# Long convolutions as 128-by-32 points in half-array tile pairs, in one phase, with the filters generated early

## The chip, the cores and the metric

The kernel runs on one core of a Trainium2 chip. The metric is the device time of one execution in microseconds (us); before the change it is 2717.03 us, the median of three runs (2716.83 to 2722.48).

## What is computed

An encoder block on 2048 tokens of 1024 columns, in float32. What matters here is the Hyena half: two-sided long filters of 4096 points for 512 channels are generated by a small network, and two long convolutions with gates follow one another.

```python
h = (z @ fw3).reshape(seq, 2, HY_ORDER, D_HY) * exp(-t * deltas)
k = concatenate([hf, 0, hb[1:][::-1]])
k = k / (sum(abs(k), axis=0) + EPS);  kf = rfft(k)            # 4096 points
z = x1 * (irfft(rfft(v, 4096) * kf[:, 0])[:2048] + v * skip[0])
z = x2 * (irfft(rfft(z, 4096) * kf[:, 1])[:2048] + z * skip[1])
```

Ahead of it stand a norm and the input projection with a recurrent unit (LRU), behind it the output projection, the router, 32 experts and the final sum.

## The kernel before, in words

The kernel is a chain of phases. Each clears its semaphores (`PhaseSemaphores.begin`), runs one instruction stream per engine, and ends when the last of its transfers has landed; nothing of the next begins before. Order inside a phase is written out by hand, with semaphores; DMAs are issued by SyncE (SP) and ScalarE (ACT), each in its own order.

1. `load_and_norm` (L83) normalizes and transposes x to `hT`, and runs the filter network's first two layers; their result `zz` goes to DRAM (L131).
2. `project_and_lru` (L226) makes 5 column groups for each of 4 channel groups (640 products of 512 columns in `fill`, L361), the short convs on DVE (`conv`, L474), the LRU, and transposes (L376) into DRAM `L`.
3. `filters` (L529) has 32 iterations of two orders: a spread of zz (POOL, L582), a generating product (PE, L609), times the decay (DVE, L660), absolute value (DVE, L663), its sum (POOL, L589), a first-stage transform (PE, L615), eviction (ACT, L639), and a store to `KA`. The reciprocals of the sums (`invn`) come last.
4. For each of two orders: `conv_forward` (L671), 16 tiles by two halves of 64-point transforms (L693), evicted to `stage` and stored to `SA` in 2 MB pieces, POOL multiplying by skip beside it (L714); `conv_blocks` (L717), 32 block transforms, each with a forward product of the signal and two of the filter (L758), two elementwise products (DVE, L803) and two inverse products (L763, L764), with matrices and data read by SP, and results stored to `SI` by ACT; `conv_inverse` (L806), which loads `SI` back in 2 MB pieces (L831), makes two products per tile (L840, L841), scales (DVE, L869), adds the skip part (POOL, L862) and gates (DVE, L876), and for the second order also squares (ACT, L902), transposes (PE, L847) and stores to `YT`.
5. `output_projection` (first DMA at L1032), `route`, `experts`, `combine`.

All transform products are full-array f32 products of 128 rows, 128 columns of weights and 512 streamed columns. Each is two LDWEIGHTS and two MATMUL records in the trace.

## Time and profile before

| | |
|---|---|
| median of 3 runs | 2717.03 us (2716.83 to 2722.48) |
| profiled execution, its own time | 2722.55 us |
| its span, mean granted clock | 2720.8 us, 0.933 |
| busy: PE, PE weight load, DVE, ACT, POOL | 2319.1, 1455.2, 1418.7, 1067.5, 316.8 us |
| DMA | 531.74 MB, 195 GB/s over the span |

The span is the time from the first to the last instruction. Busy shares are means over stages with different limits, so they are read by stage. PEclk is the granted TensorE clock as a share of full speed. In a timeline, a row gives start, busy time, engine, line, operation, output<-input and count; what stands in brackets is the idle time before it and what ended it.

### The profile page before, as it was taken

To read this page: it belongs to the slowest core of one execution; us is meant where nothing else is said; L and a number is where in the kernel's file an instruction comes from. 1 tells how busy PE (TensorE), PEld (TensorE's weight loads), DVE (VectorE), ACT (ScalarE), POOL (GpSimd) and SP (SyncE) were. 2 spreads that over 40 slices of the span, in tenths; PEclk is the share of its full clock that TensorE was granted. 3 is DMA by queue.
4 is the path that set the end of the run, shared out by engine and by line. 5 is a ranking of instruction groups with operands and counts; after the bars stand their busy time and mean duration, and the time that the engine had idled before them with its cause. 6 is when DMAs were issued, how large, how long until landed. Compare 5 with 4: busy or idle time off the path is not lost. (4 is left out here: it accounts for less than half of the span.)

```text
span 2720.8 us, 33071 instructions
## 1 busy us (share of the span) xinstructions
PE 2319.1 (85%) x8253; PEld 1455.2 (53%) x8254; DVE 1418.7 (52%) x1238; ACT 1067.5 (39%) x1342; POOL 316.8 (12%) x337
## 2 busy tenths in 40 slices
PE   2699999999879599679849994699999999999940
PEld 1344444444333244234327873588878788788830
DVE  4357291745679123312244445446486864655447
ACT  4232221414122322032222221456586965766533
POOL 0000000000078300420120000000000000000023
PEclk8899999999989799789869997799999999999975
DMA  3122313121266488378743431667598986786648
GB/s 152 34 79 64 100 47 108 33 73 58 62 214 217 173 276 280 143 276 290 276 173 111 153 136 57 246 230 290 220 388 310 395 310 240 277 309 217 261 185 355
DMA packets 263770, 531.74 MB, mean 195 GB/s; under 512 B 27311, under 2 KB 98195, under 8 KB 259347
## 3 DMA queue, kind: packets, MB, share of 16 engines
q1 hardware_dynamic: 221812, 390.76, 41.1%
q10 hardware_dynamic: 30112, 97.53, 9.0%
q0 software_dynamic: 11808, 43.00, 4.2%
q8 instruction: 17, 0.28, 0.0%
q14 instruction: 21, 0.17, 0.0%
HBM read 390.69 MB, written 140.51 MB: 195 GB/s over the span
## 5 line engine op out<-in xcount | busy, mean ns | idle before, releaser
L361 PE MATMUL pj<-hT,W 128*128 128x512 f32 x1280 | 553.7, 594 | 2.7 <-DMA W<-in_w_in_dram 2.7
L361 PEld LDWEIGHTS pj<-hT,W 128*128 128x128 f32 x1280 | 243.0, 191 | 304.3 <-issue 304.3
L1458 PE MATMUL p<-wh_hi,x_hi 128*128 128x512 f32 x768 | 309.0, 402 | 11.2 <-DVE wh_lo L1583 11.1
L1583 DVE TENSOR_TENSOR wh_lo<-w_raw,wh_hi 128x2048 fp32r<-128x2048 f32 x128 | 284.8, 2287 | 51.5 <-ACT wh_hi L1547 48.8
L1458 PE MATMUL p<-wh_lo,x_hi 128*128 128x512 f32 x768 | 304.2, 396 | 0.0
L1458 PE MATMUL p<-wh_hi,x_lo 128*128 128x512 f32 x768 | 304.1, 396 | 0.0
L1547 ACT ACTIVATE wh_hi<-w_raw 128x2048 fp32r<-128x2048 f32 x128 | 234.7, 1914 | 0.3 <-DMA w_raw<-in_exp_w_dram 0.2
L803 DVE TENSOR_TENSOR u<-pr,zs 128x512 f32<-128x512 f32 x64 | 44.3, 692 | 287.4 <-ACT zs L778 167.5
L1458 PEld LDWEIGHTS p<-wh_hi,x_hi 128*128 128x128 f32 x768 | 144.6, 188 | 49.5 <-DVE wh_lo L1583 15.0
L1458 PEld LDWEIGHTS p<-wh_hi,x_lo 128*128 128x128 f32 x768 | 144.7, 188 | 35.0
L1458 PEld LDWEIGHTS p<-wh_lo,x_hi 128*128 128x128 f32 x768 | 144.8, 189 | 32.7
L1458 PE MATMUL pyy<-wy_hi,a_hi 128*128 x392 | 160.0, 408 | 2.3 <-ACT yb L1529 2.3
L1458 PE MATMUL pyy<-wy_lo,a_hi 128*128 x392 | 155.5, 397 | 0.0
L1458 PE MATMUL pyy<-wy_hi,a_lo 128*128 x392 | 155.3, 396 | 0.0
L1583 DVE TENSOR_TENSOR wy_lo<-w_raw,wy_hi 128x2048 fp32r<-128x2048 f32 x64 | 143.6, 2285 | 0.0
L1594 DVE TENSOR_TENSOR a<-p,s 128x512 f32<-128x512 f32 x48 | 33.2, 692 | 204.2 <-ACT s L1556 204.2
L406 ACT ACTIVATE hraw<-pj 128x512 f32<-128x512 f32 x48 | 28.7, 597 | 265.1 <-PE pj L361 265.1
L1547 ACT ACTIVATE wy_hi<-w_raw 128x2048 fp32r<-128x2048 f32 x64 | 119.3, 1911 | 2.4 <-DMA w_raw<-in_exp_w_dram 1.5
L1428 POOL COPY curidx<-idx 128x1 int32 (+1 forms) x50 | 9.1, 183 | 870.3 <-PE px L1466 795.3
L1556 ACT ACTIVATE s<-p 128x512 f32<-128x512 f32 x48 | 28.9, 601 | 207.6 <-PE p L1458 207.3
L758 PE MATMUL pz<-zin,mats 128*128 128x512 f32 x128 | 67.9, 613 | 32.8 <-DMA kin<-scratch_KA 32.8
L783 ACT ACTIVATE qo<-pq 128x512 f32<-128x512 f32 x64 | 38.2, 597 | 139.0 <-PE pq L764 139.0
(266 smaller groups left out, 3796.2 us busy)
## 6 DMA issues: line engine op xcount, KB each, us to landing
w_raw<-in_exp_w_dram SPq DMA_DIRECT2D x512, 256.0 KB, 4.6
w_raw<-in_exp_w_dram SPq DMA_DIRECT2D x128, 512.0 KB, 9.6
scratch_YB<-yb ACTq DMA_DIRECT2D x50, 512.0 KB
mats<-in_mats_dram SPq DMA_DIRECT2D x64, 320.0 KB, 3.2
scratch_YB<-zero SPq DMA_DIRECT2D x4, 4096.0 KB, 14.6
scratch_KA<-kst ACTq DMA_DIRECT2D x32, 512.0 KB, 3.5
scratch_SA<-stage ACTq DMA_DIRECT2D x8, 2048.0 KB, 6.7
zin<-scratch_SA SPq DMA_DIRECT2D x64, 256.0 KB, 4.1
```

What stands on the lines that cost most here:

```text
L361: last = pe.matmul(pj[n][:, :], lhs(k), rhs(k, n), start=(k == 0), stop=(k == n_k - 1))
L406: ins = act.activation(out(n), pj[n][:, :], func)
L758: pe.matmul(bank_[s % 2][:, :], mats[:, s, m, :], rhs[:, s, :], start=True, stop=True).then_inc(fwd, 1)
L783: act.activation(qo[:, s, :], pq[s % 2][:, :], ACT.Copy).then_inc(q_evac, 1)
L803: dve.tensor_tensor(dst[:, s % 2, :], src[s % 2][:, :], zs[:, s % 2, :], ALU.mult).then_inc(uv_ready, 1)
L1428: pool.tensor_copy(cur[:, :], idx[:, ds(B + LEAD, 1)]).then_inc(idx_ready, 1)
L1458: mm = pe.matmul(acc[:, :], x[:, k, :], w, start=(k == 0 and i == 0), stop=(k == n - 1 and i == 2))
L1547: act.activation(place, raw[:, j:j + 2, :], ACT.Copy).then_inc(rounded, 1)
L1556: act.activation(s1[:, :], p1[:, :], ACT.Silu).then_inc(s_ready, 1)
L1583: dve.tensor_tensor(lo, raw[:, j:j + 2, :], hi.bitcast(F32), ALU.subtract).then_inc(lowered, 1)
L1594: dve.tensor_tensor(a[:, :], p3[:, :], s1[:, :], ALU.mult).then_inc(a_ready, 1)
```

## The change

- The 4096 points are split as N1 = 128 by N2 = 32 instead of 64 by 64. The first stage is one 128-point transform. A signal has 64 nonzero rows, so its first stage (`spread`) is two products with 64 rows each, one on partitions 0 to 63 and one on 64 to 127, into two PSUM banks. The last stage (`collect`) is two products with 64 columns of weights each, one into PSUM partitions 0 to 63 and one into 64 to 127.
- The block stage works on 16 pairs per order: for filter and signal 4 products each of 128 rows by 64 columns (2 parts by 2 halves), for the inverse 4 of 64 rows by 128 columns. The filter is transformed with the same matrix as the signal, and the complex product is done by DVE (two products of 1024 columns and a sum) and POOL (a difference). All 32 forward and 16 by 2 inverse matrices are kept on chip, loaded once.
- Both orders run in one phase, `conv`, unrolled. Collecting order 0 and spreading order 1 are interleaved tile by tile. All DMAs of the phase are issued by SP. Block data move in pieces of 256 KB, the stage in pieces of 2 MB; L is read through a ring of three 1 MB buffers.
- The skip term is added to the filter's point 0 (`norm`, `kt0`), and 1/sum is multiplied into the short conv's weights and biases, so the skip pass, the scaling and the sum on the output go.
- `filters` runs before `project_and_lru`, unrolled, on `zzd`, which `load_and_norm` leaves on chip; the absolute value goes from DVE to ACT.
- The short convs write their result in the order of even and odd positions; output projection and combine read x and write out in the matching order.

```diff
-HALF = R // 2
+N1, N2 = P, N // P
+HALF = N1 // 2
+PAIRS = N2 // 2
...
-            sp.wait_ge(mlp_sin, BASE + 3)
-            sp.dma_start(dram["ZZ"], zz[:, :]).then_inc(zz_out, 16)
...
+            act.activation(zzd[0:R, 0, :], arg[0:R, :], ACT.Sin).then_inc(mlp_sin, 1)
+            act.activation(zzd[R:P, 1, 1:SEQ][:, ::-1], arg[R:P, 1:SEQ], ACT.Sin).then_inc(mlp_sin, 1)
...
+            dve.memset(zzd[R:P, 0, :], 0.0)
+            dve.memset(zzd[0:R, 1, :], 0.0)
+            dve.memset(zzd[R:P, 1, 0:1], 0.0)
...
+            taps = PT[:, Q_HW:Q_HB, :].rearrange("p (t w) c -> p t w c", w=3)[:, :, 1:3, :]
+            step(dve.tensor_tensor(taps, taps, invn[:, :, :].unsqueeze(1).broadcast_to([P, 3, 2, CT]), ALU.mult))
+            step(dve.tensor_tensor(PT[:, Q_HB + 1:Q_HB + 3, :], PT[:, Q_HB + 1:Q_HB + 3, :], invn[:, :, :], ALU.mult))
+            by_parity = lambda a: a.rearrange("p (m g) -> p g m", g=2)
-                    conv(step, hc[:, slot, :], hraw[:, slot, :], 3, Q_HW + which, 3, Q_HB + which, hc_ready)
+                    conv(step, hc[:, slot, :].rearrange("p (g m) -> p g m", g=2), hraw[:, slot, :],
+                         3, Q_HW + which, 3, Q_HB + which, hc_ready, by_parity)
...
+def filters(nc, dram, zzd, invn):
...
+            def store(i):
+                sp.wait_ge(kst_ready, i + 1)
+                sp.dma_start(dram["KA"][:, :, order[i], :].rearrange("o p c -> p o c"), kst[:, i % 4]).then_inc(kst_out[i % 4], 16)
+            def generate(j):
+                if j >= 2:
+                    pe.wait_ge(k_ready, j - 1)
+                for o in range(2):
+                    last = pe.matmul(pk[j % 2][:, o, :], view[:, j], w3[:, o, :], start=True, stop=True)
+                last.then_inc(kgen, 1)
+            def transform(i):
+                j = order[i]
+                if j:
+                    pe.wait_ge(k_ready, j + 1)
+                else:
+                    pe.wait_ge(k0_ready, 1)
+                if i >= 2:
+                    pe.wait_ge(kst_ready, i - 1)
+                for o in range(2):
+                    last = pe.matmul(pa[i % 2][:, o, :], fa[:, :], tile(j)[:, o, :], start=True, stop=True)
+                last.then_inc(fa_done, 1)
+            generate(0)
+            generate(1)
+            for j in range(2, N2):
+                generate(j)
+                transform(j - 2)
...
+            for o in range(2):
+                pe.matmul(pk[0][:, o, :], ones[:, :], acc[:, o, :], start=True, stop=True)
+            for o in range(2):
+                for c in range(CT):
+                    place = (o * CT + c) * 2
+                    last = pe.matmul(pk[1][:, 0, place:place + 2], acc[:, o, c * P:(c + 1) * P], ones[:, 0:2], start=True, stop=True)
+            last.then_inc(norm_mm, 1)
+            transform(N2 - 1)
+            def magnitude(j):
+                act.wait_ge(k_ready, j + 1)
+                if j >= 2:
+                    act.wait_ge(summed, j)
+                act.activation(ka[:, j % 2], tile(j), ACT.Abs).then_inc(abs_ready, 1)
+            def evacuate(i):
+                act.wait_ge(fa_done, i + 1)
+                if i >= 4:
+                    act.wait_ge(kst_out[i % 4], 16 * (i // 4))
+                act.activation(kst[:, i % 4], pa[i % 2][:, :, :], ACT.Copy).then_inc(kst_ready, 1)
...
+                pool.tensor_tensor(acc[:, :, :], acc[:, :, :], ka[:, j % 2], ALU.add).then_inc(summed, 1)
...
+                dve.tensor_tensor(tile(j), pk[j % 2][:, :, :], dec[:, j % 4, :].unsqueeze(1).broadcast_to([P, 2, CH]), ALU.mult).then_inc(k_ready, 1)
...
+            dve.scalar_tensor_tensor(out=norm[:, :, :], in0=pk[0][0:1, :, :], scalar=EPS, in1=skip[:, :, :], op0=ALU.add, op1=ALU.mult).then_inc(norm_ready, 1)
...
+def conv(nc, dram, rB, ident):
...
+        def rows(a, p, t):
+            first = (p & 1) * 64 + (p >> 1 & 1) * 32 + t * 16 + (p >> 2)
+            return a[first:first + 13:4]
+            def load_k(n):
+                for t in range(2):
+                    sp.dma_start(kin[:, n % 3, t, :], rows(dram["KA"][n // PAIRS], n % PAIRS, t)).then_inc(kin_in[n % 3], 16)
+            def load_z(n):
+                for t in range(2):
+                    sp.dma_start(zin[:, n % 3, t, :], rows(dram["SA"][n // PAIRS], n % PAIRS, t)).then_inc(zin_in[n % 3], 16)
+            def store_q(n):
+                sp.wait_ge(q_evac, n + 1)
+                for t in range(2):
+                    sp.dma_start(rows(dram["SI"][n // PAIRS], n % PAIRS, t), qo[:, n % 2, t, :]).then_inc(q_out[n % 2], 16)
+            def save_stage(o, g):
+                sp.wait_ge(a_act, NT * o + 4 * g + 4)
+                sp.wait_ge(a_dve, NT * o + 4 * g + 4)
+                sp.dma_start(dram["SA"][o][:, 8 * g:8 * g + 8, :], stage[:, 8 * g:8 * g + 8, :]).then_inc(sa_out, 16)
+            def load_stage(o):
+                for s in range(2):
+                    sp.wait_ge(q_out[s], 32 * (PAIRS // 2) * (o + 1))
+                for g in range(4):
+                    sp.dma_start(stage[:, 8 * g:8 * g + 8, :], dram["SI"][o][:, 8 * g:8 * g + 8, :]).then_inc(si_in[g], 16)
+            def blocks(o):
+                sp.wait_ge(sa_out, 64 * (o + 1))
+                for n in range(o * PAIRS, o * PAIRS + 3):
+                    load_z(n)
+                for n in range(o * PAIRS, o * PAIRS + PAIRS):
+                    sp.wait_ge(z_mm, 2 * n + 2)
+                    if n + 3 < (o + 1) * PAIRS:
+                        load_z(n + 3)
+                    if n + 3 < 2 * PAIRS:
+                        sp.wait_ge(k_mm, n + 1)
+                        load_k(n + 3)
+                    if n > o * PAIRS:
+                        store_q(n - 1)
+                store_q((o + 1) * PAIRS - 1)
+            sp.dma_start(fs[:, :], dram["fa_signal"]).then_inc(tables_in, 16)
+            load_ring(0)
+            load_ring(1)
+            sp.dma_start(ia[:, :], dram["inv_a"]).then_inc(tables_in, 16)
+            load_ring(2)
+            sp.dma_start(fwd[:, :, :], dram["fwd_b"]).then_inc(fwd_in, 16)
+            for n in range(3):
+                load_k(n)
+            for g in range(GROUPS):
+                sp.wait_ge(a_mm, 8 * g + 8)
+                load_ring(g + 3)
+                save_stage(0, g)
+            sp.dma_start(inv[:, :, :, :], dram["inv_b"]).then_inc(inv_in, 16)
+            blocks(0)
+            load_stage(0)
+            for g in range(GROUPS):
+                sp.wait_ge(gated, 4 * g + 4)
+                load_ring(g + 7)
+                save_stage(1, g)
+            blocks(1)
+            load_stage(1)
+            sp.wait_ge(gated, NT + 4)
+            load_ring(11)
...
+            def spread(bank, t, src, free):
+                if free > 0:
+                    pe.wait_ge(a_act, free)
+                    pe.wait_ge(a_dve, free)
+                for g in range(2):
+                    h = slice(g * HALF, g * HALF + HALF)
+                    pe.matmul(bank[:, g, :], fs[h, :], src[h], start=True, stop=True).then_inc(a_mm, 1)
+            def k_product(n):
+                p = n % PAIRS
+                pe.wait_ge(kin_in[n % 3], 32 * (n // 3) + 32)
+                if n >= 2:
+                    pe.wait_ge(prod, 2 * n - 2)
+                for r in range(2):
+                    for t in range(2):
+                        h = slice(t * HALF, t * HALF + HALF)
+                        last = pe.matmul(pk[n % 2][h, r, :], fwd[:, 2 * p + t, r * HALF:r * HALF + HALF], kin[:, n % 3, t, :], start=True, stop=True)
+                last.then_inc(k_mm, 1)
+            def z_product(n):
+                p = n % PAIRS
+                pe.wait_ge(zin_in[n % 3], 32 * (n // 3) + 32)
+                if n:
+                    pe.wait_ge(zs_ready, 2 * n)
+                for r in range(2):
+                    for t in range(2):
+                        h = slice(t * HALF, t * HALF + HALF)
+                        last = pe.matmul(pz[h, r, :], fwd[:, 2 * p + t, r * HALF:r * HALF + HALF], zin[:, n % 3, t, :], start=True, stop=True)
+                    last.then_inc(z_mm, 1)
+            def inverse(n):
+                p = n % PAIRS
+                pe.wait_ge(yr_ready, n + 1)
+                if n:
+                    pe.wait_ge(q_evac, n)
+                for r, y, done in ((0, yr, yr_ready), (1, yi, yi_ready)):
+                    pe.wait_ge(done, n + 1)
+                    for t in range(2):
+                        h = slice(t * HALF, t * HALF + HALF)
+                        last = pe.matmul(pq[:, t, :], inv[h, p, r, :], y[h, n % 2, :], start=(r == 0), stop=(r == 1))
+                last.then_inc(inv_mm, 1)
+            def blocks(o):
+                first = o * PAIRS
+                k_product(first)
+                for n in range(first, first + PAIRS):
+                    z_product(n)
+                    if n + 1 < first + PAIRS:
+                        k_product(n + 1)
+                    if n > first:
+                        inverse(n - 1)
+                inverse(first + PAIRS - 1)
+            def collect(o, out, l, free):
+                if l % 4 == 0:
+                    pe.wait_ge(si_in[l // 4], 16 * (o + 1))
+                if free > 0:
+                    pe.wait_ge(gated, free)
+                for g in range(2):
+                    h = slice(g * HALF, g * HALF + HALF)
+                    last = pe.matmul(out[h, :], ia[:, :], stage[:, 2 * l + g, :], start=True, stop=True)
+                last.then_inc(i_mm, 1)
...
+            LAG = 2
+            for l in range(NT + LAG):
+                if l < NT:
+                    collect(0, pq[:, l % 2, :], l, l - 1)
+                if l >= LAG:
+                    t = l - LAG
+                    pe.wait_ge(gated, t + 1)
+                    spread((pz, *pk)[t % 3], t, z[:, t % 4, :], NT + t - 2 if t >= 3 else 0)
...
+            def evacuate(bank, n, t):
+                act.wait_ge(a_mm, 2 * n + 1)
+                act.activation(stage[:, 2 * t, :], bank[:, 0, :], ACT.Copy).then_inc(a_act, 1)
+            def signal(n):
+                for r in range(2):
+                    act.wait_ge(z_mm, 2 * n + r + 1)
+                    if n >= 2:
+                        act.wait_ge(prod, 2 * n - 2)
+                    act.activation(zs[:, n % 2, r, :], pz[:, r, :], ACT.Copy).then_inc(zs_ready, 1)
+            def result(n):
+                act.wait_ge(inv_mm, n + 1)
+                if n >= 2:
+                    act.wait_ge(q_out[n % 2], 32 * (n // 2))
+                act.activation(qo[:, n % 2], pq[:, :, :], ACT.Copy).then_inc(q_evac, 1)
...
+                dif = pool.tensor_tensor(yr[:, n % 2, :], by_r[:, n % 2, 0, :], by_i[:, n % 2, 1, :], ALU.subtract)
...
+                    dve.tensor_tensor(out[:, n % 2], pk[n % 2][:, :, :], zs[:, n % 2, r, :].unsqueeze(1).broadcast_to([P, 2, CH]), ALU.mult).then_inc(prod, 1)
...
+                both = dve.tensor_tensor(yi[:, n % 2, :], by_r[:, n % 2, 1, :], by_i[:, n % 2, 0, :], ALU.add)
...
+            with ExitStack() as early:
+                zzd = sb(early, "zzd", [P, 2, SEQ])
+                load_and_norm(nc, dram, hT, zzd, ident)
+                filters(nc, dram, zzd, invn)
+            project_and_lru(nc, dram, hT, invn, ident)
+        conv(nc, dram, rB, ident)
```

## Rows read from the trace of the kernel before

**Rows 1.** Busy time by stage: stretch, its length, engines, clock, DMA share, GB/s.

```profile
96.00:749.00 653.00, 628.25 (x1601) 290.00 (x1601) 354.16 (x151) 165.44 (x226) 0.93 (x3) 0.98 0.23 68
749.00:903.00 154.00, 123.69 (x260) 48.35 (x260) 132.13 (x134) 38.23 (x64) 109.34 (x98) 0.92 0.57 202
903.00:946.50 43.50, 30.23 (x64) 13.00 (x64) 0.00 (x0) 18.46 (x32) 20.31 (x16) 0.81 0.50 202
```

**Rows 2.** Timeline of TensorE in the first block phase, and that phase's middle by engine.

```profile
968.05 1.02 PE L758 MATMUL pr<-kin,mats 128*128 128x512 f32 x2
968.91 1.02 PE L758 MATMUL pi<-kin,mats 128*128 128x512 f32 x2
...
955.00:1090.00 135.00, 135.00 (x311) 59.45 (x311) 41.26 (x63) 37.02 (x62) 0.00 (x0) 0.99 0.83 275
```

**Rows 3.** Timeline at the seams of the phases, and one restart by engine.

```profile
749.70 0.34 SPq L560 DMA_DIRECT2D zz<-scratch_ZZ  x1
...
903.69 0.34 SPq L683 DMA_DIRECT2D faz<-in_fa_signal_dram  x1
...
952.90 2.07 PE L758 MATMUL pz<-zin,mats 128*128 128x512 f32 x2 [16.47 <-DMA kin<-scratch_KA]
954.76 1.91 PE L758 MATMUL pr<-kin,mats 128*128 128x512 f32 x2
...
1092.51 1.02 PE L764 MATMUL pq<-v,mats 128*128 128x512 f32 x2
1107.01 2.04 PE L840 MATMUL py<-stage,ia 128*128 128x512 f32 x2 [13.47 <-DMA stage<-scratch_SI]
...
1191.45 2.07 PE L758 MATMUL pz<-zin,mats 128*128 128x512 f32 x2 [16.33 <-DMA kin<-scratch_KA]
...
1397.54 2.12 SPq L1032 DMA_DIRECT2D wo<-in_w_out_dram  x4
...
1104.00:1109.00 5.00, 1.99 (x3) 0.99 (x4) 0.00 (x0) 0.00 (x0) 0.00 (x0) 0.50 1.01 429
```

**Rows 4.** Timeline of one iteration of the filter loop.

```profile
803.73 1.51 DVE L663 SCALAR_TENSOR_TENSOR ka<-kt 128x512 f32<-128x512 f32 x1
803.75 1.12 PE L615 MATMUL pa<-kt,fa 128*128 128x512 f32 x2 [0.35 <-DVE kt L660]
804.71 1.88 PE L609 MATMUL pk<-w,zb 128*128 128x512 f32 x4
805.57 0.19 PEld L609 LDWEIGHTS pk<-w,zb 128*128 128x128 f32 x1 [0.24 <-issue]
...
807.80 1.12 PE L615 MATMUL pa<-kt,fa 128*128 128x512 f32 x2 [0.35 <-DVE kt L660]
```

**Rows 5.** Groups of instructions: count, busy us and mean ns, idle before.

```profile
L803 DVE TENSOR_TENSOR u<-pr,zs 128x512 f32<-128x512 f32 x64 | 44.3, 692 | 287.4 <-ACT zs L778 167.5 <-PE pr L758 119.8
L500 DVE TENSOR_TENSOR Ib<-Ib,xc 128x2048 f32<-128x2048 f32 x4 | 9.2, 2294 | 0.1
L1655 ACT ACTIVATE outt<-xcomb 128x1024 f32<-128x1024 f32 x16 | 16.9, 1056 | 34.0 <-DMA out_dram<-outt 31.6 <-DVE xcomb L1671 2.3
L783 ACT ACTIVATE qo<-pq 128x512 f32<-128x512 f32 x64 | 38.2, 597 | 139.0 <-PE pq L764 139.0
L589 POOL TENSOR_TENSOR acc<-acc,ka 128x512 f32<-128x512 f32 x64 | 81.1, 1267 | 24.3 <-DVE ka L663 24.3
L1064 POOL TENSOR_TENSOR sq<-sq 128x256 f32<-128x256 f32 x16 | 11.7, 733 | 217.5 <-ACT sq L1125 217.5
```

**Rows 6.** Timeline of the start and of one channel group of the projection.

```profile
19.71 2.97 DVE L170 TENSOR_SCALAR arg<-flat,vec 128x512 f32<-128x512 f32 x4 [16.35 <-PE flat L203]
...
403.68 4.74 DVE L479 SCALAR_TENSOR_TENSOR hc<-hraw,par,hc 128x2048 f32<-128x2048 f32 x2
...
422.08 1.96 PE L376 MATMUL tr<-ident,hc 128*128 128x128 f32 x16
```

**Rows 7.** Timeline of the second inverse phase: the four transposes of one tile.

```profile
1370.78 0.60 PE L847 MATMUL pt<-ident,zn 128*128 128x128 f32 x4
```

More of the change, by code:

```diff
@@ new lines, in _ @@
+            for j in range(N2):
+                if j >= 4:
+                    sp.wait_ge(k_ready, j - 3)
+                sp.dma_start(dec[:, j % 4, :], dram["decay"][:, j, :]).then_inc(dec_in[j % 4], 16)
+                if j >= 6:
+                    store(j - 6)
+            for i in range(N2 - 6, N2):
+                store(i)
+            for s in range(4):
+                sp.wait_ge(kst_out[s], 16 * (N2 // 4))
+        @block.tensor
+        def _(pe):
+            pe.wait_ge(par_in, 16 * N_PAR)
+            view = zzd.rearrange("p h (q l) -> p l h q", l=N2)
+            def generate(j):
[20 more added lines that the diff above has]
+                transform(j - 2)
+            transform(N2 - 2)
+            pe.wait_ge(k_ready, N2)
+            pe.wait_ge(summed, N2 + 1)
+            for o in range(2):
[6 more added lines that the diff above has]
+            transform(N2 - 1)
@@ new lines, in _ @@
+        @block.scalar
+        def _(act):
+            def magnitude(j):
[8 more added lines that the diff above has]
+                act.activation(kst[:, i % 4], pa[i % 2][:, :, :], ACT.Copy).then_inc(kst_ready, 1)
+            magnitude(0)
+            magnitude(1)
+            for j in range(2, N2):
+                magnitude(j)
+                evacuate(j - 2)
+            evacuate(N2 - 2)
+            evacuate(N2 - 1)
@@ new lines, in _ @@
+            sp.dma_start(inv[:, :, :, :], dram["inv_b"]).then_inc(inv_in, 16)
[9 more added lines that the diff above has]
+            load_ring(11)
+            for t in range(NT):
+                sp.wait_ge(zt_ready, t + 1)
+                sp.dma_start(dram["YT"][t, :, 4:8, :].rearrange("p c n -> p (c n)"), zt[:, t % 2, :]).then_inc(zt_out[t % 2], 16)
@@ new lines, in _ @@
+            pe.wait_ge(tables_in, 32)
+            for l in range(NT):
+                if l % 4 == 0:
+                    pe.wait_ge(ring_in[l // 4 % 3], 16 * (l // 12) + 16)
+                spread((*pk, pz, pq)[l % 4], l, ring[:, l // 4 % 3, l % 4, :], l - 3)
+            pe.wait_ge(fwd_in, 16)
+            pe.wait_ge(a_act, NT)
+            pe.wait_ge(a_dve, NT)
+            pe.wait_ge(inv_in, 16)
+            blocks(0)
+            LAG = 2
[6 more added lines that the diff above has]
+                    spread((pz, *pk)[t % 3], t, z[:, t % 4, :], NT + t - 2 if t >= 3 else 0)
@@ new lines, in _ @@
+            pe.wait_ge(a_act, 2 * NT - 2)
+            pe.wait_ge(a_dve, 2 * NT - 2)
+            blocks(1)
+            LAG = 3
+            for l in range(NT + LAG):
+                if l < NT:
+                    collect(1, pk[l // 2 % 2][:, l % 2, :], l, NT + l - 3 if l >= 4 else 0)
+                if l >= LAG:
+                    t = l - LAG
+                    pe.wait_ge(gated, NT + t + 1)
+                    if t >= 2:
+                        pe.wait_ge(zt_ready, t - 1)
+                    for q in range(4):
+                        last = pe.transpose(pz[:, t % 2, q * P:(q + 1) * P], z[:, t % 4, q * P:(q + 1) * P], ident[:, :])
+                    last.then_inc(tr, 1)
@@ L696, in _ @@
         @block.scalar
         def _(act):
-            with act.Fori(0, NT // 4) as it:
-                for s in range(4):
-                    for h in range(2):
-                        act.wait_ge(mm, BASE + it * 8 + 2 * s + h + 1)
-                        act.activation(stage[:, h, ds(it * 4 + s, 1), :].rearrange("p a c -> p (a c)"), pa[s][h][:, :], ACT.Copy).then_inc(evac, 1)
-                act.wait_ge(evac, BASE + it * 8 + 8)
-                four = lambda a: a[:, :, ds(it * 4, 4), :].rearrange("p h l c -> p h (l c)")
-                act.dma_start(four(dram["SA"]), four(stage)).then_inc(stored, 16)
@@ new lines, in result, with blocks @@
+            def result(n):
[3 more added lines that the diff above has]
+                act.activation(qo[:, n % 2], pq[:, :, :], ACT.Copy).then_inc(q_evac, 1)
+            def blocks(o):
+                first = o * PAIRS
+                for n in range(first, first + PAIRS):
+                    signal(n)
+                    if n > first:
+                        result(n - 1)
+                result(first + PAIRS - 1)
@@ new lines, in _ @@
+            for l in range(NT):
+                evacuate((*pk, pz, pq)[l % 4], l, l)
+            blocks(0)
+            for l in range(NT):
+                evacuate((pz, *pk)[l % 3], NT + l, l)
+            blocks(1)
+            for t in range(NT):
+                act.wait_ge(gated, NT + t + 1)
+                if t:
+                    act.wait_ge(squared, t)
+                act.activation(junk[:, :], z[:, t % 4, :], ACT.Square, accum_out=ssq[:, t:t + 1]).then_inc(squared, 1)
+            act.wait_ge(ms, 2)
@@ new lines, in gate @@
+            def gate(out, t, G0, free):
+                G = G0 + t // 4
+                dve.wait_ge(i_mm, (G0 // GROUPS - 1) * NT + t + 1)
+                dve.wait_ge(ring_in[G % 3], 16 * (G // 3) + 16)
+                if t >= 4:
+                    dve.wait_ge(free, 2 * (NT + t - 3) if free is a_mm else t - 3)
+                dve.tensor_tensor(z[:, t % 4, :], out, ring[:, G % 3, t % 4, :], ALU.mult).then_inc(gated, 1)
+            for l in range(NT):
+                evacuate((*pk, pz, pq)[l % 4], l, l)
```

536 lines of the change are left out of this document (163 added, 373 removed).

## The prediction

> **What bounds the kernel now.** I read the page first: TensorE is busy for 85% of the span and no other engine for more than 52%. The table of engines by stage then shows where it is not: from 749 to 1397 us, the filters and the six conv phases, the reader sees PE short of full in the filters and, with a granted clock of 0.81, in the first forward phase, and full in the projection [rows 1]. That is the stretch the change replaces. Elsewhere it touches little. The timeline of TensorE inside a block phase gives the unit of all that follows: a f32 product of 512 columns is two MATMUL records, starts 0.858 us after the one before it, and its records end 0.16 us after the next has started [rows 2]. Five such products per transform make 4.29 us, and 32 of them 137 us: the block phases are bound by TensorE, with DMA at 0.83 of its time beside it. The gaps come next: after each block phase PE waits 13.5 us for 2 MB pieces of the stage, after each forward phase 16.4 us for the written stage to come back, and each restart, after that idle, has 4 to 6 us at a granted clock of 0.50 (the 1.2 GHz level), the first two products 1.86 us apart instead of 0.858, some 3 us lost [rows 3]. Filters: four products per tile, 3.43 us, yet a tile every 4.05 us, since the transforms wait for DVE, whose absolute-value step stretches from 0.69 to 1.5 us beside POOL's sums [rows 4].
>
> So before: filters 749.70 to 903.69 = 154.0 us; the six phases 903.69 to 1397.54 = 493.9 us [rows 3].
>
> **Filters, moved ahead of the projection.** The same 4 products per tile; the absolute value goes from DVE to ACT, POOL's two sums become one of 1024, the mask and the two extra spreads go. Per tile: PE 3.43 us; ACT two passes of 1024 at 1.06 [rows 5] = 2.1; DVE one product of 1024, by the slope between 512 (0.69) and 2048 (2.29) [rows 5] 1.2; POOL, by the slope between its 256 and 512 columns (0.73 and 1.27), 2.3 [rows 5]. PE is the last. Sum: parameters landed 4.5 us after the first issue (two w3 and fa; before it was 8, behind a MB of zz), cold start 3, 61 pairs of products up to the last generation 105, and a tail that is now in series: last sum 5, ones products 4, two one-row DVE passes and their waits 3, last transform, eviction and store 7: together 131, and 2.5 between phases. 133.5 against 154: **-20.5 us**. The weights of the generation are now read with a stride; a load takes 0.19 us in a slot of 0.43 [rows 4], and I take 0 (bounds: nothing, or 64 pairs of 0.43 = 28 us if a strided load took twice its slot). The added DVE memsets at the start lie in 16 us in which DVE waits for PE [rows 6].
>
> **Projection.** DVE's three hyena passes read every other column. At worst the first goes from 1.35 to 2.3 us (the price of 2048 columns with two inputs [rows 5]): 1 us per channel group and conv. The third conv ends at 408.4, PE's transposes of it begin at 422.1, and PE has no wait there [rows 6]: 0, covered by 14 us. Output projection and combine read and write the same 4 KB rows in another order: 0. The experts get the same counts: 0, with +/-4 for a different order.
>
> **Conv, PE.** Before, 224 products per order (32+160+32) = 192 us. After, per pair of transforms 12 products of half the array (4 filter, 4 signal, 4 inverse), 16 pairs; 32 in spread and 32 in collect: 256 per order. If two halves lie side by side that is 128 slots = 110 us; one behind the other, 220 us. No row of before shows two products side by side, so I bound it: 0.858 us per pair or 1.716. How near to 0.858? Each half is two records of 0.43 in a fixed order. If starts keep the program's order, the second half's first record starts with the first half's second: pairs of one shape still repeat every 0.858, but a run of pairs ends 0.43 late. When the shape changes (128x64 for filter, signal and collect, 64x128 for inverse and spread) the next product needs rows and columns that are still in use, so I charge 0.43 + 0.16 at each change, the 0.16 from the overlap of records [rows 2]. A pair of transforms has two changes: 6 x 0.858 + 2 x 0.59 = **6.33 us** (5.15 if a change is free). The others per pair: DVE 2 x 1.2 + 0.69 (1.5 beside POOL) = 3.1 to 3.9, ACT 2 x 0.60 + 1.06 = 2.3, POOL 1.3 to 1.5 [rows 4, 5], DMA six pieces of 256 KB = 1.57 MB, at the 275 GB/s of the block phase [rows 2] 5.7 us: all under 6.33.
>
> The Trainium skill has two sentences on this. "TensorE: Matmul & The Clock Gate", Part 3, states that matmuls on distinct row or column groups run at once (3.07x for four, 2.38x for three), but that weight loads overlap running matmuls only where the row group differs. "TensorEngine Tiling (Array Packing)", Key Properties, states that a change of tiling mode drains the array. By the first, at four for the time of 1.3, a pair would take 1.1 us and the whole 2656, an estimate from that page; the second has no price there. Against its warning on loads stands that here they lie beside full-array matmuls [rows 4]. No run here shows side-by-side halves yet.
>
> **Conv, stage by stage**, from its first DMA:
> 1. Start to first signal product: SP's queue must move 3.1 (L) + 2.1 (fwd) + 1.6 (K) + 4.2 (L) + 8.4 (SA) + 2.1 (inv) = 21.5 MB; large pieces run at 429 GB/s [rows 3], 50 us, + 3 to start and 3 for the last landing and z: 56 us. PE's 16 spread pairs (14 to 28 us) hide under it.
> 2. Blocks: 16 x 6.33 - 1.9 (first filter product done) + 3 cold + 2.6 for the last pair's chain = 105 us.
> 3. Stage back: 13.5 us, the same store, issue and first 2 MB as before [rows 3].
> 4. Collect and spread in one: per tile two shapes, 2 x (0.858 + 0.59) = 2.9 us, 46 us + 3 cold, last eviction 2, last save 5, landing 2, z 3: 61 us. DVE 1.4 and ACT 0.6 per tile are under it. DMA alone (8.4 + 12.6 MB) would need 50.
> 5. Blocks 105, stage back 13.5.
> 6. Collect with transposes: 1.45 + 0.60 + 0.16 = 2.2 per tile [rows 7], 35 us, + 3 cold, lag 3, copy and YT store 4, to the next phase 6: 51 us.
> Sum 405 against 493.9: **-89 us**. In it POOL's sums, the scaling by invn and the skip pass are gone (they hid before; the last evictions after PE, 6 us, go with them) and SI/SA gaps fall from four to two, 98 us between the block phases becoming 75.
>
> Total: 2722.55 (the profiled execution; its span is 2720.8) - 20.5 - 89 = 2613. That execution lies 5.5 over the median 2717.03, so **2608 us**.
>
> **Rivals.**
> A. As above: 2608 (2590 to 2635).
> B. Changes of shape are free: blocks 86 each (-37), step 4 bound by DMA (-12), step 6 at 1.43 per tile (-12): 2547; but then 5.15 is below the 5.7 us of DMA, +18: up to 2565. For it: at a share of 0.83 the 275 GB/s was not DMA's limit [rows 2]. Against it: the order of the four records.
> C. The loads don't run ahead across halves, so each second record waits 0.19 for its weights: 2 x (0.43 + 0.19) = 1.24 per pair, 8.24 per pair of transforms: +61, step 4 +6, step 6 +3: 2678.
> D. Column halves, which need two streams from the same 128 partitions, go in series, row halves don't: 8 x 0.858 + 0.16 + 2.31 = 9.33: +96, +7, +7: 2718, no change. Nothing in rows for or against.
> E. The other side: halves never overlap (or they do at the lower clock, the same price). 12 x 0.858 + 0.32 = 10.6 per pair of transforms: 32 x 4.3 = +137, step 4 +14, step 6 +7: **2766**. It decides at once: the change loses from about 9.3 us per pair. For it: per order 256 products against 224, and no row shows an overlap. Against it: a half uses half the rows or columns, and loads do overlap.
> F. A on a slip of the queue: everything is on SP, in order, and a wait for q_evac stands before the next z load; if loads come late by 1 us per pair, +32: 2640.
>
> **How the numbers follow.** Chances: A 0.45, B 0.12, C 0.15, D 0.06, E 0.15, F 0.07. The likeliest is 2608. The range takes A, B, C and F with 7 us beyond B and 22 beyond C for the staging sums: 2540 to 2700, leaving E and D out. A measurement of this kernel tells about 0.2% (5 us) from no change: faster 0.80 (A, B, C, F and part of D), same 0.03, slower 0.17.
>
> **What would show it.** In the block phase: one pair of transforms per 6.3 us (5.2 is B, 8.2 C, 9.3 D, 10.6 E); overlapping MATMUL records of the two halves; filters of 131 us from 100 us on; the first signal product 56 us into the conv; two stage gaps of 13.5. The projection must stay at 650 us, bound by PE. The forecast is wrong if a pair takes over 9 us, or if PE waits for DMA between pairs.

## The result, and the profile after

The changed kernel takes 3021.5 us (median of 4 runs, 3019.11 to 3024.12) beside 2719.71 us of the kernel before on the same chip (4 runs): a ratio of 1.111, interval 1.109 to 1.113. It is slower by 302 us. The forecast was 2608 (2540 to 2700), faster by 4%.

Two lines of the table of waits show where the time went (columns: total us, times, longest):

```profile
...
PE ck L803 <- DMA kin<-scratch_KA: 196.2, 26, 10.0
ACT outt L1731 <- DMA out_dram<-outt: 150.5, 14, 16.8
...
```

The first, PE's largest wait, is the block phases: 26 of 32 filter products wait for their input. The second is `combine`, where ACT waits for the output's stores. The profile splits between its stages as follows (stretch, its length, engines' busy time, clock, DMA share, GB/s; these answer to [rows 1 and 2]):

```profile
100.00:236.00 136.00, 117.57 (x276) 65.31 (x276) 44.35 (x38) 64.51 (x65) 76.32 (x35) 0.91 0.53 188
236.00:880.00 644.00, 628.86 (x1601) 290.23 (x1601) 351.81 (x152) 164.13 (x225) 0.00 (x0) 0.99 0.22 69
880.00:955.00 75.00, 20.87 (x72) 8.03 (x72) 11.07 (x16) 9.55 (x16) 0.00 (x0) 0.64 0.75 295
1000.00:1200.00 200.00, 91.20 (x280) 25.31 (x280) 33.52 (x33) 26.26 (x35) 19.44 (x11) 0.70 0.26 101
1210.00:1240.00 30.00, 30.00 (x110) 7.39 (x108) 18.28 (x27) 7.17 (x12) 0.00 (x0) 0.92 1.00 421
2800.00:3017.00 217.00, 0.00 (x0) 0.00 (x0) 63.85 (x80) 31.89 (x56) 33.13 (x26) 0.50 0.40 146
```

Filters and projection are as forecast. The block phases (fourth line) move 101 GB/s where the ones before moved 275 [rows 2], with a DMA share of 0.26, and no engine is busy for half the time. PE waits for DMA, and yet DMA's mean share over 16 engines is a quarter: it would be so if four engines always worked and twelve stood. In the last 217 us PE is idle and no engine is busy for a third of the time, at a share of 0.40.

TensorE's and SP's timeline of one pair of transforms:

```profile
1003.62 3.52 PE L803 MATMUL ck<-kin,fwd_b 128*64 128x512 f32 x8 [9.96 <-DMA kin<-scratch_KA]
1007.07 1.13 PE L826 MATMUL cq<-yr,inv_b 64*128 64x512 f32 x4
1008.03 1.02 PE L826 MATMUL cq<-yi,inv_b 64*128 64x512 f32 x4
1008.99 1.94 PE L814 MATMUL cz<-zin,fwd_b 128*64 128x512 f32 x8
1019.30 3.68 PE L803 MATMUL ck<-kin,fwd_b 128*64 128x512 f32 x8 [8.37 <-DMA kin<-scratch_KA]
```

```profile
997.54 5.18 SPq L723 DMA_DIRECT2D zin<-scratch_SA  x2
1002.77 4.92 SPq L719 DMA_DIRECT2D kin<-scratch_KA  x2
1007.73 5.54 SPq L728 DMA_DIRECT2D scratch_SI<-qo  x2
```

A pair takes 15.7 us, which is six transfers at 2.6 us. SP is held 2.5 us and more at each, where the first issue of a phase took 0.34 before [rows 3]. The products themselves are quick: the eight records of four signal products take 1.94 us, so two halves do run at once. The first filter product after the idle takes 3.5 to 3.7 us for the same eight records: PE has just stood for 8 to 10 us, and in the first pair shown the granted clock of those 3.4 us is 0.52 (the 1.2 GHz level) and 1.00 in the 4 us behind them; over the phase it is 0.70.

By stages, in the profiled executions (us; the last column is c_both below, the kernel with both kinds of transfers repaired):

| stage | before | forecast | after | repaired |
|---|---|---|---|---|
| filters (before: their phase; else: how much later the projection's first load of its weights W is) | 154.0 | 133.5 | 132.3 | 130.3 |
| conv phase in all | 493.9 | 405 | 666.2 | 360.9 |
| start to first signal product | | 56 | 73.0 | 57.9 |
| blocks, order 0 | | 105 | 225.3 | 89.2 |
| stage back | | 13.5 | 28.1 | 11.4 |
| collect and spread, to the next signal product | | 61 | 53.7 | 50.1 |
| blocks, order 1 | | 105 | 218.7 | 91.7 |
| stage back | | 13.5 | 20.4 | 11.4 |
| collect, transposes, to the next phase | | 51 | 47.0 | 49.3 |
| output projection to the end | 1323.3 | 1323.3 | 1468.4 | 1334.4 |

Each entry is the difference of two times in the timeline. The after column accounts for the whole: -21.7 + 0.9 (projection) + 172.3 + 145.1 = +296.6, the difference of the spans (3017.4 and 2720.8).

### The profile page after: what moved, and what is told of

Its sections match the earlier page's. It is cut to its first block and busy times, and to the rows that moved or that the text cites. A ratio compares the mean times of both kernels' runs of the same rounds, so it can differ in the third digit from the quotient of the medians.

```text
span 3017.4 us, 30326 instructions
## 1 busy us (share of the span) xinstructions
PE 2232.0 (74%) x8397; PEld 1388.4 (46%) x8398; DVE 1358.6 (45%) x1130; ACT 1060.3 (35%) x1262; POOL 252.5 (8%) x243
## 5 line engine op out<-in xcount | busy, mean ns | idle before, releaser
L803 PE MATMUL ck<-kin,fwd_b 128*64 128x512 f32 x256 | 104.6, 964 | 223.1 <-DMA kin<-scratch_KA 196.2
L955 DVE TENSOR_TENSOR by_r<-ck,zs 128x1024 f32<-128x1024 f32 x32 | 39.1, 1223 | 377.6 <-ACT zs L899 377.6
L1534 PEld LDWEIGHTS p<-wh_hi,x_hi 128*128 128x128 f32 x768 | 144.6, 188 | 49.5 <-DVE wh_lo L1659 15.1
L905 ACT ACTIVATE qo<-cq 128x1024 f32<-128x1024 f32 x32 | 32.8, 1024 | 364.4 <-PE cq L826 334.3
L935 POOL TENSOR_TENSOR yr<-by_r,by_i 128x512 f32<-128x512 f32 x32 | 56.6, 1769 | 1188.2 <-DVE by_i L955 1188.2
L803 PEld LDWEIGHTS ck<-kin,fwd_b 128*64 128x64 f32 x256 | 23.2, 201 | 285.8 <-DMA kin<-scratch_KA 219.1
```

Of the source, the lines that this page charges most:

```text
L803: last = pe.matmul(pk[n % 2][h, r, :], fwd[:, 2 * p + t, r * HALF:r * HALF + HALF], kin[:, n % 3, t, :], start=True, stop=True)
L905: act.activation(qo[:, n % 2], pq[:, :, :], ACT.Copy).then_inc(q_evac, 1)
L935: dif = pool.tensor_tensor(yr[:, n % 2, :], by_r[:, n % 2, 0, :], by_i[:, n % 2, 1, :], ALU.subtract)
L955: dve.tensor_tensor(out[:, n % 2], pk[n % 2][:, :, :], zs[:, n % 2, r, :].unsqueeze(1).broadcast_to([P, 2, CH]), ALU.mult).then_inc(prod, 1)
L1534: mm = pe.matmul(acc[:, :], x[:, k, :], w, start=(k == 0 and i == 0), stop=(k == n - 1 and i == 2))
```

## Theory and rivals

**Split.** A transfer is spread over no more DMA engines than the outermost dimension of its pattern has entries. The block transfers are 4 rows, 256 KB apart, of 32 by 2 KB; the output's stores and x's loads are 2 by 64 rows of 4 KB. By this theory they run on 4 and on 2 of the 16 engines, at about 25 GB/s an engine (an estimate: 64 KB in 2.6 us). The Trainium skill states this rule ("DMA: Bandwidth & Descriptors", section "Why a DMA increments its semaphore by 16 and not by 1"): the number of engines is the largest up to 16 that divides the slowest dimension larger than 1 of both patterns. It was not weighed in the forecast; the share of 0.26 agrees with it.

**Locality.** Rows that lie far apart in DRAM are slow for any engine. **Queue.** All is on SP's one queue, which serves the transfers one after the other, so 6 x 2.6 us. **PE.** The half-array products, their changes of shape and the low clock cost it.

## The experiments

Each kernel is the changed kernel with the edit shown. Times are medians, the ratio is to the kernel before on the same chip.

**The 32 outermost, the same rows** (a1_rows_outermost). The points' tables are permuted to the new row order.

```diff
-            return a[first:first + 13:4]
+            return a[first:first + 13:4].rearrange("r l c -> l r c")
-               fwd_b=full.reshape(N2, P, P).transpose(1, 0, 2), ...
+               fwd_b=full.reshape(N2, 4, N2, P).transpose(2, 1, 0, 3).reshape(P, N2, P), ...   # inv_b likewise
```

> The block phases' 256 KB transfers (filter spectrum, signal, result) keep their DRAM rows, 4 rows 256 KB apart by 32 rows of 2 KB, but are walked with the 32 as the outer dimension; the two tables that belong to that row order are permuted to match. Theory SPLIT (a transfer goes to no more engines than its outermost dimension has entries, 4 of 16, so a pair of transforms waits for 6 x 2.6 us = 15.7 us): a pair falls to PE's own time, 6 products of 0.858 = 5.2 to 6.3 us, the sum to 3021 - 32 x 9.8 = 2707, less about 15 for the first filter loads (16.4 us of issue before the signal) and about 10 for each of the two stage loads that wait behind the last stores: about 2670 (2650 to 2700). Rival LOCALITY (rows 256 KB apart in DRAM are slow, whatever engine moves them): same rows, same packets, 3021. Rival QUEUE (one queue of SP serves these transfers one after the other, 2.6 us each): 3021. Rival PE (halves and shape changes cost it): 3021.

**The rows contiguous** (a2_contiguous).

```diff
-            first = (p & 1) * 64 + (p >> 1 & 1) * 32 + t * 16 + (p >> 2)
-            return a[first:first + 13:4]
+            first = 8 * p + 4 * t
+            return a[first:first + 4].rearrange("r l c -> (r l) c")
...
-    place = (pair & 1) * 64 + (pair >> 1 & 1) * 32 + i * 4 + (pair >> 2)
+    place = pair * 8 + i
```

> The points of the transform are placed in DRAM in their natural order, so that each 256 KB transfer of a block phase is one contiguous piece, seen as 128 rows of 2 KB. SPLIT: the same as with the 32 outermost, 2670 (2650 to 2700), within 5 us of that run. LOCALITY: this one alone is fast, about 2670, and the run that keeps the strided rows stays at 3021; a part of each if it lies between. QUEUE and PE: 3021.

Measured: 2709.41 us (ratio 0.996, 0.995 to 0.998) and 2711.06 us (0.997, 0.996 to 0.998). The order in which a transfer walks its rows is worth 312 us, 10% of the kernel, with the same rows and bytes. The forecast for both had been 2670; what was counted too high is discussed below. The contiguous one is not faster than the strided one, so Locality falls; the products are untouched, so PE falls. Queue in its plain form falls too: the six transfers are still all on SP's queue, and it now takes them in 5.5 us. TensorE in the first kernel, one pair of transforms, and 60 us of its block phase:

```profile
983.88 1.94 PE L814 MATMUL cz<-zin,fwd_b 128*64 128x512 f32 x8
985.65 1.89 PE L803 MATMUL ck<-kin,fwd_b 128*64 128x512 f32 x8
987.47 1.13 PE L826 MATMUL cq<-yr,inv_b 64*128 64x512 f32 x4
...
989.38 1.94 PE L814 MATMUL cz<-zin,fwd_b 128*64 128x512 f32 x8
```

```profile
960.00:1020.00 60.00, 60.00 (x266) 19.17 (x264) 33.02 (x34) 24.26 (x33) 19.48 (x11) 1.00 0.84 277
```

A pair now takes 5.50 us, PE is busy for all of it at full clock, and DMA moves 277 GB/s.

**Result stores on ACT's queue** (e_result_on_act).

```diff
                 act.activation(qo[:, n % 2], pq[:, :, :], ACT.Copy).then_inc(q_evac, 1)
+                act.wait_ge(q_evac, n + 1)
+                for t in range(2):
+                    act.dma_start(rows(dram["SI"][n // PAIRS], n % PAIRS, t), qo[:, n % 2, t, :]).then_inc(q_out[n % 2], 16)
...   # store_q and its calls on SP are left out
```

> The result stores of the block phases are issued by ACT in place of SP, with their 4 x 32 rows as they are. SPLIT: the same bytes on the same 4 engines, a pair still takes 15.7 us, 3021 +-15. QUEUE: SP keeps 4 of 6 transfers of a pair, 10.5 us, and ACT has the others beside it: 3021 - 32 x 5.2 = 2855.

Measured: 3025.66 us (1.113, 1.111 to 1.114), where the changed kernel has 1.111. Its filter products in TensorE's timeline, over four pairs (one row left out):

```profile
991.91 3.53 PE L795 MATMUL ck<-kin,fwd_b 128*64 128x512 f32 x8 [3.43 <-DMA kin<-scratch_KA]
1011.51 3.68 PE L795 MATMUL ck<-kin,fwd_b 128*64 128x512 f32 x8 [12.28 <-DMA kin<-scratch_KA]
1022.97 3.36 PE L795 MATMUL ck<-kin,fwd_b 128*64 128x512 f32 x8 [3.76 <-DMA kin<-scratch_KA]
...
1054.03 3.68 PE L795 MATMUL ck<-kin,fwd_b 128*64 128x512 f32 x8 [3.67 <-DMA kin<-scratch_KA]
```

The rhythm changes (11 and 20 us by turns), the mean does not: (1054.03 - 991.91) / 4 = 15.5, and 15.7 over eight pairs. A second queue brings nothing. The phase moves 102 GB/s at a share of 0.26, as before:

```profile
1000.00:1160.00 160.00, 76.77 (x240) 20.99 (x240) 33.40 (x33) 21.87 (x32) 18.19 (x11) 0.72 0.26 102
1016.66 8.21 SPq L719 DMA_DIRECT2D kin<-scratch_KA  x2
```

Beside ACT's stores SP is held 4.1 us at each filter load, where it was 2.5: both queues draw on one capacity, which by Split is that of the same four engines. Queue falls.

**Two doses** (d_loads_wide, d_stores_wide). `wide` is the order of the first experiment, used for the four loads of a pair alone, or for the two stores alone (with the one table that belongs to it).

```diff
-                    sp.dma_start(zin[:, n % 3, t, :], rows(dram["SA"][n // PAIRS], n % PAIRS, t)).then_inc(zin_in[n % 3], 16)
+                    sp.dma_start(zin[:, n % 3, t, :], wide(dram["SA"][n // PAIRS], n % PAIRS, t)).then_inc(zin_in[n % 3], 16)
...   # kin's loads and fwd_b's row order likewise
```

> Dose: only the four loads of a pair are walked with 32 outermost, the two result stores keep 4 x 32 rows; output and x as in the changed kernel. SPLIT with 25 GB/s for each engine (64 KB in 2.6 us): the four lowest engines carry 2 x 64 KB of stores and 4 x 16 KB of loads, 5.2 + 2.6 = 7.8 us per pair of transforms, the others 2.6; a pair takes 7.8, 2.3 above the 5.5 of the kernel with all six wide: 2709 + 32 x 2.3 = 2783 (2765 to 2800). If stores on few engines are hidden by the buffers: 2709. If any narrow transfer holds the queue: 5.2 + 4 x 0.65 is the same number, so the period alone does not tell those two apart.

> The other dose: the two result stores are walked with 32 outermost, the four loads keep 4 x 32 rows. SPLIT: 4 x 2.6 + 2 x 0.65 = 11.7 us per pair: 2709 + 32 x 6.2 = 2907, and 14 more for the six first filter loads, 2920 (2895 to 2935). If only the loads count, because PE waits for them: 15.7 less nothing, 3021; if the time went by the number of narrow transfers in another proportion, the two doses together tell it.

Measured: 2780.61 us (1.023, 1.021 to 1.024), forecast 2783; and 2910.58 us (1.071, 1.070 to 1.073), forecast 2920. The filter products with wide loads start every 7.7 us (7.8 was worked out), with wide stores every 11.95 (11.7):

```profile
1003.85 1.94 PE L806 MATMUL ck<-kin,fwd_b 128*64 128x512 f32 x8 [0.29 <-DMA kin<-scratch_KA]
1011.58 1.94 PE L806 MATMUL ck<-kin,fwd_b 128*64 128x512 f32 x8 [2.00 <-DMA kin<-scratch_KA]
1019.28 1.94 PE L806 MATMUL ck<-kin,fwd_b 128*64 128x512 f32 x8 [1.98 <-DMA kin<-scratch_KA]
```

```profile
1010.48 3.68 PE L806 MATMUL ck<-kin,fwd_b 128*64 128x512 f32 x8 [4.74 <-DMA kin<-scratch_KA]
1022.41 3.42 PE L806 MATMUL ck<-kin,fwd_b 128*64 128x512 f32 x8 [3.94 <-DMA kin<-scratch_KA]
1034.40 3.68 PE L806 MATMUL ck<-kin,fwd_b 128*64 128x512 f32 x8 [4.79 <-DMA kin<-scratch_KA]
```

The periods fit the load of the busiest DMA engine: bytes on that engine over 25 GB/s. A service of one transfer after the other, at 2.6 us a narrow and 0.65 us a wide one, whichever queue it came from, would give the same periods, and no run tells the two apart. With no, 2, 4 and 6 narrow transfers of six it is 5.50 (PE is last there), 7.7, 11.95 and 15.7 us.

**Output and x in halves** (b_out_halves).

```diff
-                sp.dma_start(out_t[ds(t, 1)].rearrange("a g n d -> (a g) n d"), out[:, q % 2, :]).then_inc(o_out[q % 2], 16)
+                for g in range(2):
+                    sp.dma_start(out_t[ds(t, 1), g].rearrange("a n d -> (a n) d"), out[64 * g:64 * g + 64, q % 2, :]).then_inc(o_out[q % 2], 16)
...   # the three loads of x and the counts that are waited for likewise
```

> The store of the output (512 KB, walked as 2 x 64 rows of 4 KB) and the load of x in the output projection are each made as two transfers of 64 rows; nothing else changes. SPLIT (outermost dimension 2, so 2 engines, 10 us per 512 KB, two stores in flight): the last product of the experts' first kind to the end falls from 234.7 us to the 120 of before, the output projection from 236 us of PE to the 227 of before: 3021 - 115 - 10 = 2896 (2885 to 2910). LOCALITY (rows of 4 KB that lie 128 KB apart are slow): 3021. QUEUE: 32 transfers more on SP at 0.3 to 0.5 us, 3021 to 3035.

Measured: 2887.42 us (1.062, 1.060 to 1.064), 134 below the changed kernel, where 125 were expected. The products of the output projection (first to last `pA`) took 226.1 us before, 236.7 after the change, 226.0 here; from the last expert product of the first kind to the end it is 119.8, 249.5 and 126.3. (The 234.7 us of the expectation were counted from a later mark than its 120, hence its 115 for a gain of 123.) The chain that ended last in the changed kernel has these among its longest pieces (start, length):

```profile
2848.27 23.10 DMA out_dram<-outt
...
2903.22 22.91 DMA out_dram<-outt
```

Two stores are in flight, so one 512 KB tile ends every 13.7 us (four in the 54.8 us between the two ends, 2871.37 and 2926.13). The dose rule gives that nearly: each of two engines carries 256 KB of the store and a sixteenth of the tile's 1.5 MB of loads, 360 KB at 25 GB/s = 14 us. Two engines that always work and fourteen that are busy for 3.9 of 13.7 us make a share of 0.37, where 0.40 was read above. The rows still lie 128 KB apart in the repaired stores, so it was not their distance either.

**Both repairs** (c_both).

> Both repairs in one kernel: the block phases' transfers walked with 32 outermost, and the output's stores and x's loads as halves of 64 rows. SPLIT: the two places are apart in time and share nothing, so the gains add: 3021 - 312 - 134 = 2575 (2568 to 2585). A rival, SHARED (both took the same waiting out, for instance a clock that recovers once): less than the sum, 2600 or more.

Measured: 2578.44 us (5 runs; ratio 0.949, 0.948 to 0.951), forecast 2575. The gains add. This beats the kernel before by 139 us and the changed one by 443. TensorE is busy throughout the middle of the block phases (their last inverse product waits 2.3 us for POOL), and ACT's wait for the output falls from 150.5 to 39.3 us:

```profile
960.00:1020.00 60.00, 60.00 (x264) 19.08 (x262) 33.54 (x33) 23.73 (x34) 19.27 (x11) 1.00 0.84 278
```

```profile
ACT outt L1735 <- DMA out_dram<-outt: 39.3, 14, 5.1
```

**The inverse table later** (g_inverse_table_later), on top of both repairs.

```diff
-            sp.dma_start(inv[:, :, :, :], dram["inv_b"]).then_inc(inv_in, 16)
             blocks(0)
...
                 for n in range(o * PAIRS, o * PAIRS + 3):
                     load_z(n)
+                if not o:
+                    sp.dma_start(inv[:, :, :, :], dram["inv_b"]).then_inc(inv_in, 16)
...   # PE waits for inv_in at its first inverse product
```

> As the kernel with both repairs, and the 2.1 MB table of the inverse is issued behind the first six signal loads instead of ahead of them, and waited for at the first inverse product. If DMA sets the first signal product (28.6 us of PE waiting there), 2.1 MB at the 342 to 429 GB/s of that stretch are 5 to 6 us: 5 us below the kernel with both repairs. If the written stage's way back sets it, 0. If the first inverse then waits for the table instead, 0 to 2 us less.

Measured: 2578.32 us (0.949, 0.947 to 0.950), no change. SP's first signal load is issued 49.4 us after the phase's first DMA in both kernels (930.24 - 880.79 and 931.52 - 882.17): the written stage's way back sets it, and the table never delayed it. PE then begins with the signal instead of waiting for the table:

```profile
935.18 3.68 PE L815 MATMUL cz<-zin,fwd_b 128*64 128x512 f32 x8 [24.03 <-DMA zin<-scratch_SA]
938.65 3.17 PE L804 MATMUL ck<-kin,fwd_b 128*64 128x512 f32 x8
...
945.67 1.13 PE L829 MATMUL cq<-yr,inv_b 64*128 64x512 f32 x4 [0.42 <-DMA inv_b<-in_inv_b_dram]
```

The first signal product is 4.8 us earlier after the phase's first DMA (53.0 against 57.9), the first inverse product only 2.0 (63.5 against 65.5), since it waits for the table; 2 us can't be told in the total.

**Neighbours on the same half** (f_halves_unpaired), on top of both repairs: in the filter and signal products the loops over r and t are exchanged (and ACT hears of the signal's first part one product later).

```diff
-                for r in range(2):
-                    for t in range(2):
+                for t in range(2):
+                    for r in range(2):
...   # z_mm is raised in the second half only
```

> As the kernel with both repairs, but the four filter products and the four signal products of a pair are ordered half by half: both of the left columns' half, then both of the right's, so that neighbours use the same half. SIDE BY SIDE in program order (a product starts when its half is free and the one before it has started): the first of a group is alone, the second and third go together, the fourth goes with the first of the next group; a pair of transforms gets one slot of 0.86 longer, 5.5 to 6.4 us, 32 x 0.86 = 27 us, 2606 (2590 to 2620). LOOK AHEAD (the array takes what is free in any order): 5.5 us, 2578. NO OVERLAP of neighbours at all except in pairs: 2 x 0.858 a group for 2 groups more, 8.9 us, 2688.

Measured: 2586.19 us (0.951, 0.950 to 0.953). That is 8 us above c_both, with intervals that touch. A pair takes 5.55 us, from 1001.08 to 1006.63 in its timeline, against 5.50, 1.6 us over 32 pairs. The profiled executions are 8.9 us apart, of which 2.1 lie ahead of conv and 2.5 behind it, where the edit touches nothing; conv is 4.2 longer (365.1), 4.6 in the block phases, where the last inverse products wait for POOL 0.85 us longer each.

```profile
1001.08 1.94 PE L814 MATMUL cz<-zin,fwd_b 128*64 128x512 f32 x8
1002.85 1.94 PE L803 MATMUL ck<-kin,fwd_b 128*64 128x512 f32 x8
...
1006.63 1.94 PE L814 MATMUL cz<-zin,fwd_b 128*64 128x512 f32 x8
```

The program order in which a start must wait for the one before it, which the forecast had assumed, would have made it 6.4; Side by side in that form falls. The halves overlap in either order.

## Why the prediction was wrong, point by point

**The failed step.** "DMA six pieces of 256 KB = 1.57 MB, at the 275 GB/s of the block phase [rows 2] 5.7 us: all under 6.33." The 275 GB/s came from transfers of 128 rows in one dimension. The diff gives the new ones another shape: `rows` returns a slice of 4 by 32 rows. They ran at 101 GB/s, 15.7 us a pair. In the two block phases that is 444 us against 181 repaired; with the stages next to them (the first filter loads, held 16 us in SP's queue, and stage reads that wait for the last stores) it accounts for 305 of conv's 666. SP's queue in the changed kernel and with the rows outermost (a1_rows_outermost), at the six filter loads ahead of the first signal:

```profile
886.32 16.36 SPq L719 DMA_DIRECT2D kin<-scratch_KA  x6
```

```profile
886.66 3.89 SPq L719 DMA_DIRECT2D kin<-scratch_KA  x6
```

A rate read from a row holds for the shape of that row, and the shape is what the step should have compared. With both kinds of transfers repaired the kernel takes 2578.44 us, 30 under the forecast and inside its range.

**The same failure again.** "Output projection and combine read and write the same 4 KB rows in another order: 0." The rows are the same, the outer dimension is 2 instead of 128: 134 us (b_out_halves).

**Filters, -20.5.** Right. The projection's first load of its weights W, on SP's queue, moves from 105.05 to 237.37, +132.3 where 133.5 was forecast, and the phase of 154.0 is gone. PE is last with 3.43 us a tile, which answers to the 4.05 of [rows 4]:

```profile
140.21 1.88 PE L604 MATMUL fp<-kt,fa 128*128 128x512 f32 x4
...
143.64 1.45 PE L604 MATMUL fp<-kt,fa 128*128 128x512 f32 x3
```

The other engines were sized well from [rows 5]: DVE's product 1.224 us (1.2), ACT's pass 1.056, POOL's sum 2.356 (2.3). The strided weight load, priced at 0 within bounds of 0 and 28 us, takes 298 ns instead of 194, in a slot of 430, and is hidden:

```profile
L592 PEld LDWEIGHTS fk<-w,zzd 128*128 128x128 f32 x128 | 38.0, 298 | 29.7 <-issue 8.9 <-DMA skip<-in_hy_skip_dram 8.4 <-DVE kt L663 0.4
L604 PEld LDWEIGHTS fp<-kt,fa 128*128 128x128 f32 x128 | 24.7, 194 | 30.1 <-issue 22.8 <-DVE kt L668 2.6 <-DVE kt L663 0.8
```

**Projection, 0.** Right: 645.5 against 644.7 us from its first weight load to the next phase. The fear for the short convs was idle; the pass that starts them takes 1.347 us with every other column, as without:

```profile
L482 DVE TENSOR_SCALAR hc<-hraw,par x12: 1345/1347/1347, 299.4 to 847.8; 128x2048 f32<-128x2048 f32 x12
L482 DVE TENSOR_SCALAR xc<-xraw,par x4: 1346/1346/1347, 271.8 to 741.2; 128x2048 f32<-128x2048 f32 x4
```

**PE's unit, 6.33 us.** The mechanism (halves side by side) held, the price of a shape change was too high. A pair is 6 x 0.858 = 5.15 and 0.35 for its changes, not 1.18: 5.50. Collect and spread together take 2.07 us per tile, 1.72 + 0.35, where 2.9 was charged. That is nearest to rival B. Its bounds for conv (405 - 61, and 18 more for DMA) are 344 to 362, and the repaired kernel has 360.9; that this fits is in part luck, since the 18 us for DMA never came (PE is last at 5.50 us a pair), while the last collect has 49.3 us where B took 12 off 51. Rivals C, D and E, the ways in which halves would not overlap, fell, and two half products took 0.858 us together, not the 1.1 of the estimate in the prediction.

```profile
1217.89 1.08 PE L847 MATMUL cq<-stage,ia 128*64 128x512 f32 x4
1218.90 1.13 PE L793 MATMUL ck<-z,fs 64*128 64x512 f32 x4
1219.96 1.08 PE L847 MATMUL cq<-stage,ia 128*64 128x512 f32 x4
```

**Staging.** Start to the first signal product: 56 forecast, 57.9 repaired. Stage back: 13.5 against 11.4. Collect and spread 61 against 50.1, the last collect 51 against 49.3. The first two terms stand. Collect and spread were 11 us too high by the changes of shape above. The last collect fits by luck: a tile takes 1.60 us instead of 2.2, some 10 us less, and PE then stands 7.7 us in the middle of it, since DVE's copy waits for the store of an earlier tile to `YT`:

```profile
1210.92 0.69 DVE L998 COPY zt<-cz 128x512 f32<-128x512 f32 x1 [9.20 <-DMA scratch_YT<-zt]
1211.76 1.09 PE L885 MATMUL cz<-ident,z 128*128 128x128 f32 x4 [7.65 <-DVE zt L998]
```

**The other side.** E was to cost through PE; what happened is nearest to F, transfers that come late, which was priced at 1 us per pair and cost 10. "The forecast is wrong if PE waits for DMA between pairs" was the sign, and it is the first line of PE's waits; at 15.7 us a pair the other sign stands too.

**Not foreseen, small.** The repaired kernel's part from the output projection on is 11 us longer than before (1334.4 against 1323.3): 3.5 between the last projection product and the first expert product, 5.3 from the experts' last to the end, 1.6 at the projection's start, and 0.8 in the experts themselves, well within their range of 4. In `combine`, 32 stores of 256 KB stand in place of 16 of 512; that these cost it was not tried.

In the first two experiments 2670 was expected and 2709 measured. 32 pairs at 9.8 us less were to give 313 us; by the table the block phases gave 225.3 - 89.2 + 218.7 - 91.7 = 263. In the changed kernel they are 444 us and not 32 x 15.7 = 502, since some transfers of a phase lie outside it, such as the signal loads of its first three pairs, which are issued before it begins. The stages around them gave 44 (15.1 + 16.7 + 9.0 + 3.6) where 35 was expected. (These differences are read from c_both, and taken to hold for the first experiment.)

## What to carry to other kernels

For every transfer that a change adds or reshapes, write down its outermost dimension on both sides before taking a rate from another row: put a large one there (32, 64 and 128 entries were fast here; permute the tables, or cut the transfer into pieces of 64 rows), and if it must be narrow, price it as bytes on its busiest engine over 25 GB/s. In a profile, a wait for DMA beside a DMA share of a quarter, and SP held for microseconds at an issue, points to that fault; another queue did not mend it here. The other half of the lesson is that the change itself was good: the shapes of two sets of transfers hid a gain of 139 us behind a loss of 302.

## What the runs showed of the hardware

- The same 256 KB took 2.6 us as 4 by 32 rows (101 GB/s, DMA share 0.26) and at most 0.92 us with 32 outermost (six in 5.50 us). Read as four engines at 25 GB/s each, an estimate since no view shows a single engine, this gave 7.8, 11.7 and 14 us where 7.7, 11.95 and 13.7 were measured.
- SP is held at each issue of the narrow transfers: 2.5 to 2.8 us, against 0.6 to 0.7 in the repaired phase (1.21 to 1.42 us for two).
- Row halves and column halves of f32 products overlapped, the column halves in either order of the program (5.50 and 5.55 us a pair, six slots of 0.858 being 5.15), and a change between them cost 0.17 us.
- DMA at 1.57 MB per 5.50 us (286 GB/s; the rows of 60 us show 277 and 278) ran beside a PE that was busy all the time.
- A weight load that reads every 32nd column took 298 ns instead of 194.
